# Down projections of two gated feed-forward layers as seven block products per pair of output tiles

## The reference

```
# first block
h = rms_norm(x, norm2_g)
u = depthwise_conv(h @ w_up, up_conv_w, up_conv_b, 1, 1)     # 3 taps along the sequence
gate, val = split(u, 2)                                      # 3072 channels each
x = x + (gelu(gate) * val) @ w_down                          # 3072 -> 1024
x = rms_norm(x, final_g)
# second block
h = rms_norm(x, norm_ffn_g)
gate, up = split(h @ w_ffn_in, 2)                            # 2816 channels each
x = x + (silu(gate) * up) @ w_ffn_out                        # 2816 -> 1024
out = rms_norm(x, final_norm_g)
```

## Time and profile before

| | |
|---|---|
| median of three runs | 3456.22 us (3455.56 to 3456.25) |
| profiled execution, its own time | 3458.81 us |
| span of its instructions | 3457.0 us, granted clock 0.991 |
| PE busy | 3363.4 us, 97% |
| DVE / ACT / POOL busy | 2208.1 / 1435.4 / 1123.1 us |
| up stages in the trace | 560 to 965 us and 2770 to 3165 us (about) |
| down stages | 965 to 1285 us and 3165 to 3457 us (about, with the norms behind them) |

### The profile page before, as it was taken

One profiled execution on the slowest core, in us unless ns is written; L12 is line 12 of the kernel. 1 busy time (PEld: TensorE's weight loads), 2 busy tenths in 40 slices (PEclk: granted clock), 3 DMA queues, 4 the chain that ended last, 5 costly groups with the idle time before them and its releaser, 6 DMA issues.

```text
span 3457.0 us, 44808 instructions
## 1 busy us (share of the span) xinstructions
PE 3363.4 (97%) x16634; PEld 2711.7 (78%) x16634; DVE 2208.1 (64%) x2247; ACT 1435.4 (42%) x1901; POOL 1123.1 (32%) x644
## 2 busy tenths in 40 slices
PE   9999899999999999999999999999889999999998
PEld 6677777888888868888887777777667878888886
DVE  8996968777773474322277888888856564444434
ACT  5688835444441142333223443344453353333213
POOL 2000028888832212111111111111112376766222
PEclk9999999999999999999999999999999999999999
DMA  4210221222252112111111110111122212223322
GB/s 143 62 44 19 73 90 67 81 85 79 85 195 95 48 43 92 36 42 36 37 49 43 37 42 31 42 42 36 43 79 85 79 63 90 76 88 122 134 89 82
DMA packets 59167, 242.52 MB, mean 70 GB/s; under 512 B 6592, under 2 KB 6592, under 8 KB 53312
## 3 DMA queue, kind: packets, MB, share of 16 engines
q1 hardware_dynamic: 59072, 241.22, 19.7%
HBM read 194.53 MB, written 41.42 MB: 68 GB/s over the span
## 4 chain that ended last, share of the span: by engine, by line
PE 81%; DVE 13%; issue 3%; ACT 3%; DMA 0%; POOL 0%; DVEq 0%; POOLq 0%; ACTq 0%
PE ps L508 45%; PE ps L1459 24%; PE ps L2699 2%; PE ps L2711 2%; PE ps L2688 1%; PE ps L2849 1%; PE ps L2862 1%; DVE conv_acc L2312 1%; DVE t_wide L1096 1%; PE ps L531 1%; PE ps L2801 1%; PE ps L2856 1%; PE ps L2835 1%; DVE small L2352 1%; PE ps L2797 1%
## 5 line engine op out<-in xcount | busy, mean ns | idle before, releaser
L479 POOL TENSOR_TENSOR w_lo_part<-w_raw,w_hi_part 128x1024 fp32r<-128x1024 f32 x162 | 404.7, 2498 | 1736.3 <-ACT w_hi_part L462 1736.3
L508 PE MATMUL ps<-h_hi_part,w_hi_part 128*128 128x512 f32 x1904 | 623.5, 408 | 30.1 <-DVE h_lo_part L1632 12.0
L508 PE MATMUL ps<-h_lo_part,w_hi_part 128*128 128x512 f32 x1904 | 594.7, 393 | 0.0
L508 PE MATMUL ps<-h_hi_part,w_lo_part 128*128 128x512 f32 x1904 | 593.1, 392 | 0.0
L462 ACT ACTIVATE w_hi_part<-w_raw 128x1024 fp32r<-128x1024 f32 x180 | 189.1, 1051 | 719.5 <-PE ps L508 631.7
L508 PEld LDWEIGHTS ps<-h_hi_part,w_hi_part 128*128 128x128 f32 x1904 | 346.4, 190 | 126.0 <-issue 41.6
L508 PEld LDWEIGHTS ps<-h_hi_part,w_lo_part 128*128 128x128 f32 x1904 | 360.5, 189 | 78.2
L508 PEld LDWEIGHTS ps<-h_lo_part,w_hi_part 128*128 128x128 f32 x1904 | 360.6, 189 | 78.0 <-issue 0.3
L2312 DVE SCALAR_TENSOR_TENSOR conv_acc<-u_pad,cols,conv_acc 128x1024 f32<-128x1024 f32 x232 | 307.3, 1325 | 19.4 <-DVE conv_acc L2312 2.7
L2151 DVE TENSOR_TENSOR residual<-residual,ps 128x1024 f32<-128x1024 f32 (+1 forms) x60 | 73.2, 1220 | 268.0 <-PE ps L508 267.9
L508 PE MATMUL ps<-u_hi,w_hi_part 128*128 128x512 f32 x736 | 232.0, 390 | 0.0
(11 more groups left out here) (449 smaller groups left out, 6596.8 us busy)
## 6 DMA issues: line engine op xcount, KB each, us to landing
w_raw<-in_w SPq DMA_DIRECT2D x226, 512.0 KB, 3.3
w_raw_odd<-in_w SPq DMA_DIRECT2D x46, 512.0 KB, 3.8
u_spill<-ffn_u SPq DMA_DIRECT2D x46, 512.0 KB, 3.0
u_wide<-u_spill SPq DMA_DIRECT2D x23, 1024.0 KB, 9.1
residual<-in_x SPq DMA_DIRECT2D x4, 1024.0 KB, 10.5
both_halves<-q_chan SPq DMA_DIRECT2D x16, 256.0 KB, 4.4
x_again<-in_x SPq DMA_DIRECT2D x8, 512.0 KB, 3.9
residual<-in_x SPq DMA_DIRECT2D x2, 2048.0 KB, 7.2
```

The lines of the kernel that those rows point to most:

```text
L479: pool.tensor_tensor(WLO[:, slot], WRAW[:, slot], f32(WHI[:, slot]), ALU.subtract).then_inc(w_ready, 1)
L508: last = pe.matmul(PS[:, ps, b * HALF:(b + 1) * HALF], st[:, slot, k, :], at(mv, k, b), start=(k == 0 and n == 0), stop=(k == nk - 1 and n ...
```

## The change

The down projections go through the pipeline of the up projections, as twelve more "pairs" behind the 24 (or 22): three groups of input channels, in each four pairs of output tiles (`OUT_PAIRS`).

- Eleven of the twelve are made by seven products, of 4 channel tiles each (3 in the last group of f = 1). The last is direct: eight half products, on two outputs of each half of the sequence.
- The activation operands of a group are seven quadrants of u: `b11`, `b21`, `b22`, and `t1` to `t4`, which are differences. VectorE makes the differences as u is made, three instructions after every second pair (`sums`), and all eight quadrants are stored. Each operand is loaded over the low part of the one before, once the product that used it last is done (`part`), and split in place: four high parts of 512 columns on ScalarE (`down_hi_act`), four low parts on VectorE (`down_lo_dve`), instead of one instruction of 1024 columns per tile.
- The seven products are not added up in PSUM: VectorE adds seven partial results of 512 columns per pair to X straight from PSUM (`add_down`), where it added two of 1024. The weight arrays are laid out anew by the host.
- GpSimd's and ScalarE's work on weights is that of an up pair, for each of the twelve. The order of all of it is written out in `up_act`, `up_dve`, `up_pe` and `up_sync`.
- The squares for the norms behind the down projection move from the last group to the end.

The core of the diff, for VectorE and TensorE (`up_dve`, `up_pe`):

```diff
+            def sums(p):
+                if not p.odd():
+                    return
+                ...
+                dve.tensor_tensor(to[:, 0:2, :], U8[:, 1:2, :].broadcast_to([P, 2, HALF]), U8[:, 0:4:3, :], ALU.subtract
+                                  ).then_inc(u_sums, 1)
+                dve.tensor_tensor(to[:, 2, :], U8[:, 3, :], to[:, 0, :], ALU.subtract).then_inc(u_sums, 1)
+                dve.tensor_tensor(to[:, 3, :], U8[:, 2, :], to[:, 2, :], ALU.subtract).then_inc(u_sums, 1)
...
                 if m.conv:
                     made(c + -1)
-                if more:
-                    dve.wait_ge(up_lo, split_at("s1", c + 1) + m.steps)
-                    up_sum_one(dve, m, c + 2, 0)
+                    sums(c + -1)
+                sum_first(c + 2)
...
+            cycle(At(n - 2))
+            lower(0, "b11")
+            scaled(p)
+            lower(0, "b21")
+            lower(0, "t1")
+            gate_taps(p)
+            read("x1", n)
+            if not m.conv:
+                made(p)
+            val_taps(p)
+            c22(At(n - 1))
+            if m.conv:
+                made(p)
+            lower(0, "t2")
+            read("y", n)
+            sum_first(At(n + 1))
+            read("z1", n)
+            lower(0, "t3")
+            p = At(n - 1)
+            scaled(p)
+            read("x2", n)
+            lower(0, "t4")
+            read("x1", n + 1)
+            sum_first(At(n + 2))
+            lower(0, "b22")
+            read("x3", n)
+            gate_taps(p)
+            read("y", n + 1)
+            val_taps(p)
+            read("z1", n + 1)
+            made(p)
+            read("x4", n)
+            sums(p)
+            read("z2", n)
+            for c in range(n + 1, ns - 1):
+                d = c - n
+                g = d // 4 + 1
+                read("x2", c)
+                if d % 4 == 0:
+                    lower(d // 4, "t4")
+                read("x1", c + 1)
+                if c + 2 < ns:
+                    sum_first(At(c + 2))
+                if d % 4 == 0:
+                    lower(d // 4, "b22")
+                read("x3", c)
+                if d % 4 == 3:
+                    lower(g, "t2")
+                read("y", c + 1)
+                read("z1", c + 1)
+                if d % 4 == 2 and g < 3:
+                    lower(g, "b11")
+                if d % 4 == 3:
+                    lower(g, "t3")
+                read("x4", c)
+                if d % 4 == 2 and g < 3:
+                    lower(g, "b21")
+                read("z2", c)
+                if d % 4 == 2 and g < 3:
+                    lower(g, "t1")
+        def down_lo_dve(dve, m, g, name, last=False):
+            ...
+            for k in range(m.ks(g)):
+                dve.wait_ge(down_hi, m.part_at[i] + k + 1)
+                dve.tensor_tensor(m.lo[slot][:, k, :], m.wide[slot][:, k, :], f32(m.hi[slot][:, k, :]), ALU.subtract
+                                  ).then_inc(down_lo, 1)
+            c = At(n - 1)
+            ...
+            pe.wait_ge(c21_read, m.g + n - 1)
+            down_product(pe, m, "a11", n, x_bank(m, n), True)
+            ...
+            for c in range(n, m.ns - 1):
+                seen("x1", c)
+                down_product(pe, m, "s2", c, x_bank(m, c), False)
+                if c == n:
+                    pe.wait_ge(c21_read, m.g + n)
+                else:
+                    seen("x4", c - 1)
+                down_product(pe, m, "a11", c + 1, x_bank(m, c + 1), True)
+                seen("x2", c)
+                down_product(pe, m, "s3", c, x_bank(m, c), False)
+                seen("y", c)
+                down_product(pe, m, "a12", c + 1, BANK_Y, True)
+                ...
+                down_product(pe, m, "s1", c + 1, z_bank(m, c + 1), True)
+                seen("x3", c)
+                down_product(pe, m, "a22", c, x_bank(m, c), False)
+                seen("z1", c)
+                down_product(pe, m, "s4", c, z_bank(m, c), False)
```

And the end of the stage for f = 0 (`two_norms_dve`, then `up_pe`):

```diff
+            st.do(dve.memset(SS2[:, :], 0.0))
+            for k in range(2):
+                square_dve(dve, 2, k)
+            down_lo_dve(dve, m, 2, "b12", True)
+            for k in range(2, 4):
+                square_dve(dve, 2, k)
+            add_down(dve, m, "x3", last)
+            st.do(dve.memset(SSB[:, :], EPS * EPS * D / P))
+            square(0, 0)
+            add_half(dve, m, "l0")
+            square(1, 1)
+            add_down(dve, m, "x4", last)
+            square(2, 2)
+            square(3, 3)
+            ...
+            for k in range(4, 7):
+                square(k, k, 0)
+            down_lo_dve(dve, m, 2, "b22", True)
+            add_half(dve, m, "l1")
+            square(7, 7, 0)
...
+            down_product(pe, m, "s2", c, x_bank(m, c), False)
+            half_product(pe, m, "a11", "b11", 0, True)
+            seen("x2", c)
+            down_product(pe, m, "s3", c, x_bank(m, c), False)
+            half_product(pe, m, "a12", "b21", 0, False)
+            seen("x3", c)
+            down_product(pe, m, "a22", c, x_bank(m, c), False)
+            half_product(pe, m, "a21", "b11", 2, True)
+            half_product(pe, m, "d22", "b21", 2, False)
+            seen("z1", c)
+            down_product(pe, m, "s4", c, z_bank(m, c), False)
+            if m.f == 0:
+                second_sum_pe(pe, 0)
+            ... four more half products, then the sum of the right half
```

More of the change, by code:

```diff
@@ L49 @@
 J_OUT = 18
-J_FFN = J_OUT + 8
-J_F = J_FFN + 24
+J_F = J_OUT + 8
 J_GLA = J_F + 2
@@ new lines, in up_sync @@
+            part(0, "b11", n)
+            part(0, "b21", n)
+            u_store(At(n - 3))
+            part(0, "t1", n)
+            sp.wait_ge(c11_read, m.g + n)
+            x_load(0, 0, 1)
+            x_load(0, 3, 4)
+            next_raw(At(n - 1))
+            part(0, "t2", n)
+            part(0, "t3", n)
+            u_store(At(n - 2))
+            part(0, "t4", n)
+            part(0, "b22", n)
+            sp.wait_ge(c12_read, m.g + n)
+            x_load(1, 1, 3)
+            next_raw(At(n))
@@ L1404, in up_dve, with sum_first, cycle @@
             scale_dve(dve, st, LEFT)
-            def cycle(c, more=True):
+            def sum_first(q):
+                dve.wait_ge(up_lo, split_at("s1", q + -1) + m.splits)
+                up_sum_one(dve, m, q, 0)
+            def cycle(c):
                 scaled(c + -1)
@@ L1444, in up_dve, with read, lower @@
-            for g in range(2):
-                for k in range(8):
-                    if g or k:
-                        down(g, k)
-                    if 8 * (g + 1) + k < n:
-                        u_lo_dve(dve, m, g + 1, k)
-        def product(pe, m, op, q, to, first, fresh=False, inc=1):
+                    sums(c + -1)
+                sum_first(c + 2)
+            def read(what, q):
+                add_down(dve, m, what, q)
+            def lower(g, name):
+                down_lo_dve(dve, m, g, name)
@@ L1675, in two_norms_act @@
             f_upper(0)
+            for k in range(6, KT):
+                square(k)
             for k in range(3, KT):
```

823 lines of the change are left out of this document (472 added, 351 removed).

## The result

The changed kernel takes 3552.55 us (median of 4, 3551.59 to 3556.05) against 3455.89 us (median of 4, 3455.0 to 3456.25) for the kernel before on the same chip: 1.0279 times, 95% interval 1.0266 to 1.0291. That is slower, as forecast, but by 96.7 us where I had 25.8, and 42 us above the top of the range.

What follows compares the result with a forecast made beforehand. The prediction took PE to bound the kernel, with VectorE, blocked by GpSimd, making it wait in the down stages. Terms -55.7 + 1 + 27 + 9 + 27 + 12.5 + 5 = +25.8 us gave 3482 us, range 3432 to 3510.

Steps and rivals of the forecast that it cites:

- What bounds the kernel, and what PE saves: Whole kernel: PE is nearly always full, so 255 fewer matmuls at 0.2278 us save 55.7 us.
- The price of a blocked instruction: VectorE instructions with two SBUF inputs: one GpSimd instruction costs each 1.09 us, 1.782 instead of 0.692.
- Up stages: Up stage of f = 0: the added differences cost 1 us, bounds 0 and 16; f = 1: 0.
- GpSimd the bound: Rival, first up stage: GpSimd falls 1 us a cycle behind, 15 us in all, time 3497; chance 0.12.
- Entry, f = 0: Start of the down pairs, f = 0: VectorE's 52 us of work plus blocking makes it 27 us late; bounds 6 and 34.
- Changes of group: Two per down stage: reads behind blocked low parts cost 7.4 us each, three times, then 4.8; 27 us, bounds 0 and 45.
- loads late: Rival, changes of group: slower operand loads cost 2 us for each of four changes, time 3490; chance 0.05.
- Ends: End of each down stage: squares no longer hidden cost 12.5 us in f = 0 (6 to 18), 5 in f = 1 (2 to 9).
- all upper bounds together: Every term at its upper bound: 3537 us, called unlikely all at once.
- The signs: Down stage f = 0: gapless 19.1 us pairs mid-group, PE waits at named reads, 10 us or more ahead of the norm.
- DVE above 8 tenths there: Sign for the down stage of f = 0: VectorE busy above 8 tenths, 512-column low parts averaging 1.2 to 1.5 us.
- VectorE keeps up: Rival, all stages: low parts rarely meet GpSimd instructions, costs total 36 us, time 3436; chance 0.25.

Runs made afterwards that it cites:

- pool_narrow: Changed kernel with GpSimd making only 2 of 128 columns per channel tile in weight sums and six of seven low parts of each down pair: 3461.1 us, 1.0011 times before.

## Why the prediction was right in sign and wrong in size

**What bounds the kernel, and what PE saves.** Right: 255 matmuls fewer, and in the down stages every wait of PE but one of 1.17 us is for VectorE.

**The price of a blocked instruction.** Right. The low parts have a mean of 1.20 us, at the edge of the 1.2 to 1.5 that was named, and pool_narrow shows 0.65 with most of GpSimd's instructions cut short: 91.5 of 96.7 us go away with them. What earlier weights have in it isn't parted; VectorE's idle time for them, 11 us at the changes and entries, is my estimate of the most that they hold, besides slow matmuls.

**Up stages: mis-sized, 8.3 for 1.** The step that failed is "w_sum is then no longer blocked, so it ends 2.6 later", "hidden, with 0.6 to spare". One cycle, VectorE and then GpSimd, against the earlier trace rows:

```profile
706.22 2.09 DVE L1563 TENSOR_TENSOR ffn_u<-ffn_u 128x1024 f32<-128x1024 f32 x1
708.34 1.67 DVE L1566 TENSOR_TENSOR ffn_u<-ffn_u 128x512 f32<-128x512 f32 x1
710.04 0.69 DVE L1568 TENSOR_TENSOR ffn_u<-ffn_u 128x512 f32<-128x512 f32 x1
710.65 0.69 DVE L1002 TENSOR_TENSOR w_sum<-w_raw 128x512 f32<-128x512 f32 x1
...
711.85 0.68 DVE L1519 TENSOR_TENSOR ffn_val<-ps,ffn_rstd 128x512 f32<-128x512 f32 x1
```

```profile
705.26 1.97 POOL L987 TENSOR_TENSOR a_lo<-w_raw,a_hi 128x512 fp32r<-128x512 f32 x1 [0.27 <-ACT a_hi L976]
707.39 2.07 POOL L987 TENSOR_TENSOR a_lo<-w_raw,a_hi 128x512 fp32r<-128x512 f32 x1 [0.16 <-POOL a_lo L987]
711.50 1.29 POOL L1002 TENSOR_TENSOR w_raw<-w_raw 128x512 f32<-128x512 f32 x1 [2.04 <-DVE w_sum L1002]
```

Two of the three differences met a GpSimd instruction (2.09 and 1.67 us), so they took 4.4 us, not 3.7. The scaling L1519 ended at 712.5 and `a11` waited 0.62 us (712.67 on PE's timeline). Every second cycle repeats that: two cycles take 39.2 us instead of 38.3. Once blocking is at work, a margin of 0.6 us is none. The rival (GpSimd the bound) had the right place and half the price, but the wrong engine: GpSimd is idle 2.04 us here.

**Entry, f = 0: right in place, and in size by luck**, 29.6 for 27, with waits at the places that were named, and 6.19 us at the first where 5 to 6 stood. But nearly 8 of the 29.6 are slow matmuls and edges of waits, which the sum didn't have, and the waits alone (21.8 us) were less than forecast. The two errors cancel.

**Changes of group: the largest miss, 15.6 for 7.4, and 63.0 for 27 over the four.** The waits alone are 46 us, above the upper bound of 45, and slow matmuls add the rest. Waits of 5.27 and 6.09 us stand where 5.4 and 2 were said, and the slow matmuls behind both add 4.2. The second was forecast too short because the low parts of b22 were given an average blocking, and because a load was left out. VectorE before that wait, in the kernel after:

```profile
1127.16 1.25 DVE L1002 TENSOR_TENSOR w_sum<-w_raw 128x512 f32<-128x512 f32 x1 [1.55 <-DMA w_raw<-in_w]
1128.33 6.78 DVE L1181 TENSOR_TENSOR b_lo<-b_wide,b_hi 128x512 fp32r<-128x512 f32 x4
```

All four are blocked, 1.70 us each, and `w_sum` had first waited 1.55 us for its weights, whose load was issued only at 1122.18. That load was nowhere in the sum; it makes 1.55 of the 4.1 us that the second wait is over its forecast, and 3.78 us of idle VectorE stand at the last change of f = 1. The operand loads were in the sum: they land in 5.4 and 5.2 us (median) where 4.5 were estimated, and none of them stands in the chain that ended last at a change, so the rival *loads late* is out for u there. For the weights, which it didn't name, it holds.

**Ends: mis-sized**, 21.5 for 12.5 and 15.9 for 5. The left sum waits 10.28 us (11.6 forecast), but the wait for the third norm's sum (6.66 us) and the slow matmuls weren't in it.

**A term that was missing: the clock.** This is the step that failed most widely: a wait was priced at its own length, and the matmuls behind it at 0.2278 us. Some 30 of the 68 us between forecast and account are slow matmuls. The rows of before had a hint, a clock of 0.99 in the down stretch with the norms in it. The prediction named six waits of 4 us or more one by one (one at each entry, three at changes, the left sum); with 2 us added to each the sum would have been 12 us higher. Since no bound had this term either, even all upper bounds together (3537) lie below the 3552.6 that were measured.

**The signs.** The places of the waits came as said. "DVE above 8 tenths there" didn't: VectorE is busy 206.4 of 297 us in the down stage of f = 0, 0.69. It has room in the middle of the groups, and is late at their changes all the same.

**The chances.** Slower had 0.63. The rival "VectorE keeps up" fell, and further than I thought: it gave 3436 us for less than half of the blocking, and pool_narrow, with next to none, takes 3461.

## What to carry to other kernels

A saving on an engine that never stops costs more than its waits as soon as waits appear: gaps of 3.65 us and more in TensorE cost some 2 to 3 us above their own length here, and shorter ones close behind another gap cost 1.6. Where VectorE and GpSimd both work on SBUF, count the time during which either holds the other up (here 1.20 us a low part, and 0.65 with GpSimd's instructions cut short) as one engine's time, and move an operation to the engine that makes it faster, even if that one is the fuller: three sums a pair gave 28 us here. When an instruction is made later, look at who stores its result: SyncE's issues, in a fixed order, carried the delay to the loads behind it here (21 of 24 us came back when the store was moved), and after one such store has been moved there may be a second. And when a narrow kernel takes the bound away, look at what its remaining waits stand behind before calling them the engine's: here most of them stood behind loads.

## What the runs showed of the hardware that I had not expected

Behind a gap of only 3.65 us TensorE's granted clock was 0.50 for 3.3 us, with a matmul every 0.43 us in place of 0.227, and over gaps from 3.65 to 16.77 us the loss behind them was 1.8 to 2.9 us. A gap of 2.72 us, 11 us after one of 3.28, did it too, while gaps of 3.27, 3.28 and 3.39 us did not. VectorE's low parts, one behind the other, were blocked one by one: four took 1.70 us each, beside four instructions of GpSimd of 1.43 to 1.59 us in the same stretch. Three sums a pair moved from GpSimd to the more loaded VectorE made the kernel 28 us faster.
